# Attention values with V as the weight operand, the two head groups in the two halves of the array's columns

## What is computed

```python
def block_attn(args):                      # one block of 128 queries, all heads
    i, qb, ib = args
    ...
    s_s = jnp.einsum('bqgrd,bgqkd->bqgrk', qb, ksel)
    p_s = masked_softmax(s_s, smask)
    o_s = jnp.einsum('bqgrk,bgqkd->bqgrd', p_s, vsel)
    ...
    s_w = jnp.einsum('bqgrd,bkgd->bqgrk', qb, kwin)
    p_w = masked_softmax(s_w, wmask[None, :, None, None, :])
    o_w = jnp.einsum('bqgrk,bkgd->bqgrd', p_w, vwin)
    return o_s, o_w
...
out = g[..., 0:1] * o_cmp + g[..., 1:2] * o_sel + g[..., 2:3] * o_win
```

## Time and profile before

| | us |
|---|---|
| median of 3 runs | 1659.43 |
| lowest, highest | 1656.99, 1665.18 |
| span of the profiled execution | 1660.4 |
| attention phase: first score matmul to last values matmul | 607.0 to 911.2 |
| PE busy in the whole span | 1436.3 (87%) |

### The profile page before, as it was taken

How to read it: one execution, slowest core, us unless ns; L and a number is a source line. 1 busy time by engine, 2 the same in 40 slices (tenths; PEclk the granted TensorE clock), 3 DMA queues, 4 the chain that set the end, 5 groups by cost and what they waited for, 6 DMA issues and landing times. The chain is left out here.

```text
span 1660.4 us, 17595 instructions
## 1 busy us (share of the span) xinstructions
PE 1436.3 (87%) x6162; PEld 885.5 (53%) x6182; DVE 573.4 (35%) x1140; ACT 402.3 (24%) x990; POOL 193.0 (12%) x242
## 2 busy tenths in 40 slices
PE   4899999999967768999999599999729999999980
PEld 2445544554534667788887255566514444444440
DVE  0234223323345326655554113334551111111115
ACT  1121112111112534554443013233201111111110
POOL 0012012201210002111100000000011110110104
PEclk8899999999988658999999699999859999999995
DMA  9110001001207620100040310210155999999948
GB/s 366 47 38 26 19 32 38 25 13 38 64 31 260 230 70 26 52 27 27 24 193 8 118 51 4 73 39 26 39 177 189 366 372 364 372 371 365 370 151 304
DMA packets 125755, 224.16 MB, mean 135 GB/s; under 512 B 6016, under 2 KB 82048, under 8 KB 125568
## 3 DMA queue, kind: packets, MB, share of 16 engines
q1 hardware_dynamic: 118640, 197.69, 33.9%
q0 software_dynamic: 7056, 25.69, 4.1%
HBM read 181.42 MB, written 41.94 MB: 135 GB/s over the span
## 5 line engine op out<-in xcount | busy, mean ns | idle before, releaser
L432 PE MATMUL pj<-arena,xT 128*128 128x512 f32 (+1 forms) x768 | 318.5, 572 | 2.2 <-DMA arena<-in_w_in 2.0
L432 PEld LDWEIGHTS pj<-arena,xT 128*128 128x128 f32 x768 | 146.3, 194 | 155.4 <-issue 150.2
L1709 PE MATMUL egu<-arena,exT 128*128 128x512 f32 x512 | 227.6, 598 | 1.2 <-issue 1.2
L1709 PEld LDWEIGHTS egu<-arena,exT 128*128 128x128 f32 x512 | 95.7, 192 | 110.4 <-issue 109.8
L1108 DVE TENSOR_REDUCE anm<-asc 128x1 f32<-128x640 f32 (+7 forms) x128 | 90.5, 707 | 121.9 <-PE asc L1012 121.2
L1069 ACT ACTIVATE ap<-asc,anm 128x640 f32<-128x640 f32 (+7 forms) x128 | 89.7, 701 | 157.9 <-DVE anm L1108 147.4
L1697 PE MATMUL eyp<-arena,ehT 128*128 128x512 f32 x256 | 115.2, 593 | 1.0 <-ACT ehT L1740 1.0
L1267 PE MATMUL xpj<-arena,xTA 128*128 128x512 f32 x256 | 113.9, 604 | 0.7 <-ACT xTA L1334 0.7
L233 ACT ACTIVATE raw<-pj 128x512 f32<-128x512 f32 (+1 forms) x48 | 27.1, 564 | 271.9 <-PE pj L432 271.9
L1767 DVE TENSOR_TENSOR eh<-esg,egu 128x256 f32<-128x256 f32 x32 | 13.5, 421 | 220.2 <-ACT esg L1746 220.2
L1023 PE MATMUL atp<-early,ap 128*128 128x128 f32 x528 | 82.9, 281 | 5.1 <-ACT apT L1080 4.4
(11 more groups left out here) (321 smaller groups left out, 1978.2 us busy)
## 6 DMA issues: line engine op xcount, KB each, us to landing
arena<-in_w_gate SPq DMA_DIRECT2D x32, 1024.0 KB, 7.5
arena<-in_w_up SPq DMA_DIRECT2D x32, 1024.0 KB, 9.8
arena<-in_w_down SPq DMA_DIRECT2D x32, 1024.0 KB, 11.6
y_d<-ey SPq DMA_DIRECT2D x32, 512.0 KB, 9.9
arena<-in_w_in SPq DMA_DIRECT2D x6, 2048.0 KB, 18.6
x<-in_x SPq DMA_DIRECT2D x16, 512.0 KB, 4.2
y_d<-arena SPq DMA_DIRECT2D x2, 4096.0 KB, 18.7
rope<-in_rope SPq DMA_DIRECT2D x8, 512.0 KB, 3.5
```

Of the source, the lines that this page charges most:

```text
L432: last = nc.tensor.matmul(dst[:, 0:n], xT[:, k, :], w[c][:, k, :], start=k == 0, stop=k == KT - 1)
L1709: last = nc.tensor.matmul(gu[k % 2][:], xT[k % 2][:, c, :], m.gateup[k][:, c, :], start=c == 0, stop=c == KT - 1)
```

## The change

The product of probabilities and V is turned round. V is now the weight operand, 64 columns wide, and the transposed probabilities, 128 columns, move. The output is therefore transposed too: channels on partitions, queries along the row. A head of group 0 writes partitions 0 to 63 of `aov[branch]` and the head of group 1 at the same place p in its group writes partitions 64 to 127, so the two are products in different halves of the array's columns, and they are issued in turns (block 0 of group 0, block 0 of group 1, block 1 of group 0, ...).

For that the list of units changes: head pairs p = 0 to 3, and for each pair selected group 0, selected group 1, window group 0, window group 1. `values` handles two units at a time: PE does scores(u), turn(u - 2), and at even u values of units u - 4 and u - 3. `apT` has four buffers instead of two (two lie in `m.kcvcT`).

Because the output is transposed, it has to be turned back once a tile: `keep` copies `aov[0]` (ACT) and `aov[1]` (DVE) to `m.middle`, behind exponential or maximum of the tile's fourth unit (of the next tile) and ahead of the copies of unit u - 2; `turn_back` (PE) transposes the eight 128x128 blocks into two further pieces of `atp`, in the iteration after; `gates` reads those pieces instead of `aov`, two units later than before. Per-branch semaphores `a_kept` take the place of `a_read`, `a_free` that of `a_evac`.

```diff
 def attention_units():
 
     for i in range(NT):
-        for h in range(NH):
-            yield i, h, 0, 0, i + 1
-            yield i, h, 1, max(0, i - 4), min(i + 1, 5)
+        for p in range(HPG):
+            for branch, k0, n in ((0, 0, i + 1), (1, max(0, i - 4), min(i + 1, 5))):
+                for g in range(NG):
+                    yield i, g * HPG + p, branch, k0, n
...
-        pT = [sb(f"apT{b}", [P, NT, P]) for b in range(2)]
+        pT = [sb(f"apT{b}", [P, NT, P])[:] for b in range(2)]
+        pT += [m.kcvcT[:, b].rearrange("p (k q) -> p k q", k=NT) for b in range(2)]
+        oT = [m.middle[:, 512 * b:512 * b + 512] for b in range(2)]
...
+        first_piece, back_piece, f = {}, {}, 0
+        for u in range(U + 3):
+            if u < U:
+                first_piece[u] = f
+                f += len(pieces[u])
+            i, since = divmod(u - 2, PER)
+            if i >= 1 and since == 0:
+                back_piece[i - 1] = f
+                f += 2
+        after = lambda u: first_piece[u] + len(pieces[u])
...
-                def values(u):
-                    i, h, branch, k0, n = units[u]
+                def turn_back(i):
+
+                    for branch in range(2):
+                        f = back_piece[i] + branch
+                        pe.wait_ge(kept[branch], i + 1)
+                        pe.wait_ge(freed[f % 2], f // 2)
+                        for p in range(HPG):
+                            last = nc.tensor.transpose(tp[f % 2][:, p * P:(p + 1) * P],
+                                                       oT[branch][:, p * P:(p + 1) * P], m.c("ident"))
+                        last.then_inc(s["turned"], 1)
+
+                def values(j):
+
+                    i, p, branch, k0, n = units[2 * j]
                     v = m.vw if branch else m.vs
-                    g = h // HPG
-                    f = first_piece[u + 1]
-                    pe.wait_ge(s["evac0"], (f + 1) // 2)
-                    pe.wait_ge(s["evac1"], f // 2)
-                    if h == 0 and i:
-                        pe.wait_ge(s["read"], 2 * i)
+                    f = after(2 * j + 1)
+                    pe.wait_ge(freed[0], (f + 1) // 2)
+                    pe.wait_ge(freed[1], f // 2)
+                    if p == 0 and i:
+                        pe.wait_ge(kept[branch], i)
                     for b in range(n):
-                        at = (k0 + b) * P + g * HD
-                        last = nc.tensor.matmul(ov[branch][:, h * HD:(h + 1) * HD], pT[u % 2][:, b, :],
-                                                v[:, at:at + HD], start=b == 0, stop=b == n - 1)
+                        for g in range(NG):
+                            at = (k0 + b) * P + g * HD
+                            last = nc.tensor.matmul(ov[branch][g * HD:(g + 1) * HD, p * P:(p + 1) * P],
+                                                    v[:, at:at + HD], pT[(2 * j + g) % 4][:, b, :],
+                                                    start=b == 0, stop=b == n - 1)
                     last.then_inc(s["valued"], 1)
 
-                for u in range(U + 3):
+                for u in range(U + 5):
                     if u < U:
                         scores(u)
                     if 2 <= u < U + 2:
                         turn(u - 2)
-                    if u >= 3:
-                        values(u - 3)
-
...
+            def evacuate(eng, copy, u, parity):
                 for j, (k, n) in enumerate(pieces[u]):
                     f = first_piece[u] + j
                     if f % 2 == parity:
                         eng.wait_ge(s["turned"], f + 1)
-                        if u >= 2:
-                            eng.wait_ge(s["valued"], u - 1)
-                        copy(pT[u % 2][:, k:k + n, :],
-                             tp[f % 2][:, 0:n * P].rearrange("p (k q) -> p k q", k=n)).then_inc(sem_, 1)
+                        if u >= 4:
+                            eng.wait_ge(s["valued"], u // 2 - 1)
+                        copy(pT[u % 4][:, k:k + n, :],
+                             tp[f % 2][:, 0:n * P].rearrange("p (k q) -> p k q", k=n)).then_inc(freed[parity], 1)
+
+            def keep(eng, copy, i, branch):
+                eng.wait_ge(s["valued"], NH * (i + 1))
+                if i:
+                    eng.wait_ge(s["turned"], back_piece[i - 1] + branch + 1)
+                copy(oT[branch][:], ov[branch][:]).then_inc(kept[branch], 1)
...
+                copy = lambda o, a: nc.scalar.activation(o, a, ACT.Copy)
+                for u in range(U + 4):
                     if u < U:
                         softmax(u)
-                    if u >= 2:
-                        evacuate(act, lambda o, a: nc.scalar.activation(o, a, ACT.Copy), u - 2, 0, s["evac0"])
+                    i, since = divmod(u - 3, PER)
+                    if i >= 1 and since == 0:
+                        keep(act, copy, i - 1, 0)
+                    if 2 <= u < U + 2:
+                        evacuate(act, copy, u - 2, 0)
...
-                    dve.wait_ge(s["valued"], PER * (i + 1))
...
-                    nc.vector.tensor_tensor(heads(t1[:]), heads(ov[0][:]), bc(w[b][:, 0:8].unsqueeze(2), [P, NH, HD]),
-                                            ALU.mult).then_inc(s["read"], 1)
-                    nc.vector.tensor_tensor(heads(t2[:]), heads(ov[1][:]), bc(w[b][:, 8:16].unsqueeze(2), [P, NH, HD]),
-                                            ALU.mult).then_inc(s["read"], 1)
+                    for branch, t in enumerate((t1, t2)):
+                        f = back_piece[i] + branch
+                        dve.wait_ge(s["turned"], f + 1)
+                        nc.vector.tensor_tensor(
+                            t[:].rearrange("p (g h d) -> p g h d", g=NG, h=HPG),
+                            tp[f % 2][:].rearrange("p (h g d) -> p g h d", g=NG, h=HPG),
+                            bc(w[b][:, 8 * branch:8 * branch + 8].rearrange("p (g h o) -> p g h o", g=NG, o=1),
+                               [P, NG, HPG, HD]), ALU.mult).then_inc(freed[f % 2], 1)
...
-                for u in range(U + 3 + STEPS):
+                copy = lambda o, a: nc.vector.tensor_copy(o, a)
+                for u in range(U + 5 + STEPS):
                     if u < U:
                         maximum(u)
+                    i, since = divmod(u - 3, PER)
+                    if i >= 1 and since == 0:
+                        keep(dve, copy, i - 1, 1)
                     if 2 <= u < U + 2:
-                        evacuate(dve, lambda o, a: nc.vector.tensor_copy(o, a), u - 2, 1, s["evac1"])
-                    i, since = divmod(u - 2, PER)
+                        evacuate(dve, copy, u - 2, 1)
+                    i, since = divmod(u - 4, PER)
```

More of the change, by code:

```diff
@@ L947, in phase_attend @@
         pieces = [[(k, min(4, n - k)) for k in range(0, n, 4)] for _, _, _, _, n in units]
-        first_piece = [0]
-        for p in pieces:
-            first_piece.append(first_piece[-1] + len(p))
-        ocv = m.oc_d.rearrange("(t p) d -> t p d", p=P)
         U = len(units)
         PER = 2 * NH
+        first_piece, back_piece, f = {}, {}, 0
[8 more added lines that the diff above has]
+        after = lambda u: first_piece[u] + len(pieces[u])
+        ocv = m.oc_d.rearrange("(t p) d -> t p d", p=P)
         with nc.Block() as block:
@@ L1046, in _ @@
                         turn(u - 2)
-                    if u >= 3:
-                        values(u - 3)
-            def evacuate(eng, copy, u, parity, sem_):
+                    i, since = divmod(u - 4, PER)
+                    if i >= 1 and since == 0:
+                        turn_back(i - 1)
+                    if u >= 4 and u % 2 == 0 and u - 4 < U:
+                        values((u - 4) // 2)
+            def evacuate(eng, copy, u, parity):
                 for j, (k, n) in enumerate(pieces[u]):
@@ L1065, in softmax @@
                     if u >= 2:
-                        act.wait_ge(s["turned"], first_piece[u - 1])
+                        act.wait_ge(s["turned"], after(u - 2))
                     if h == 0 and i >= 2:
@@ L1131, in finish @@
                     if step == 1:
-                        dve.wait_ge(s["read"], 2 * i + 2)
+                        for branch in range(2):
+                            f = back_piece[i] + branch
+                            dve.wait_ge(freed[f % 2], f // 2 + 1)
                         done(nc.vector.tensor_tensor(t1[:], t1[:], t2[:], ALU.add))
```

8 lines of the change are left out of this document (5 added, 3 removed).

## The result

The changed kernel takes 1669.97 us in the median (1657.22 to 1676.33, 20 runs). The kernel before, in the same runs, takes 1656.93 (1651.14 to 1665.18, 20 runs). The ratio is 1.0077, with a 95% interval of 1.006 to 1.0095: slower by 13 us, where the forecast was 1668.3 and slower by 0.5% or a little more.

What follows compares the result with a forecast made beforehand. PE's own queue was taken to set the attention's pace before the change, with turns then waiting on ACT's copies. Terms -5 - 5.2 + 15.5 + 1 + 1.6 = +7.9 on 1660.4 gave 1668.3 us, range 1658 to 1680.

Steps and rivals of the forecast that it cites:

- part 1: Value matmuls: two streams run side by side in the array's halves, so 113 us become 56.5.
- The rival in which the halves take turns: Value matmuls: halves take turns or loads don't hide, 56 us more on PE, 1700 to 1725; chance 0.07.
- part 2: Around each of 64 values groups: entering and leaving the half-array form costs 0.3 us, 19 us in all.
- part 3: Turns in tiles 4 to 7 wait for ACT's copy to free `atp`; with the halved values, together -5.2 us.
- part 4: Seven tile borders: stalls and transposes for turning back, 19.7 us less 4.2 that go, +15.5 us.
- the gates' 4.2: Tile borders: the 4.2 us the first values waited for the gates in six borders before, expected to go.
- the pitch's 1.6: Value matmuls: the moving side at 0.11 instead of 0.107 on 528 steps adds 1.6 us.
- a rival of its own: Attention: border stalls and half-array products bring the lower clock, 1680 to 1695 us; chance 0.16.
- One sign of being wrong: Attention: a granted clock of 0.5 after tile 1, listed among what would show the forecast wrong.
- The cover holds: Attention turns don't wait, so PE's work decides: 30 us less, 1630 to 1648; chance 0.12.
- Borders are cheap: Tile borders: transposes back slip in without the 2 us stalls, sum -5, 1655 us; chance 0.09.
- the first list: Signs of being right: turn waits some 1.8 us, values groups 1.9 to 2.1, border idle about 2, copy waits near 45.

Runs made afterwards that it cites:

- the pair of kernels without stalls: New unit order with the old product, and the changed kernel without the turn back, both with ACT copying ahead of the exponential: 1646.62 and 1607.9 us.
- the second profile: The changed kernel, unedited, run and profiled once more: 1665.76 us, ratio 1.0054 to the kernel before.
- The swap: ACT's copy of unit u - 2 put ahead of the exponential of unit u: 1616.87 us on the changed kernel, 1643.26 on the kernel before.
- Kernels with half-array products and no stalled turns: The changed kernel with ACT copying ahead of the exponential, with and without the turn back: 1616.87 and 1607.9 us.
- a kernel with full-array products and the stalls: Kernel before with the new unit order, four apT buffers and values two units at a time, old product, no turn back: 1698.42 us, ratio 1.0258.

## Why the prediction was right

**What bounds.** The reading that ACT's copy, not PE's work, would set the pace holds: taking its cause away gives 49 to 53 us, and PE had 25 us less to do in a phase that grew.

**The values (part 1).** Taken: 0.107 to 0.11 for two instructions side by side. Measured 0.055 an instruction. The rival in which the halves take turns is out for the kernel as changed; it comes nearly true when the program order doesn't alternate. The Trainium skill (TensorE: Matmul & The Clock Gate, The mechanism) has weight loads overlap only where the row group differs. Here both halves use all rows and 32 matmuls with a load each still take 1.90 where the old form takes 3.49; the measurement decides.

**The change of form (part 2).** Taken 0.3 a group. The line through the two groups (1.24 for 20, 1.90 for 32) leaves 0.14 at none; and from a turn of 5 to the values are 0.67 (895.23 to 895.90) where the earlier trace rows have 0.57. That is 0.24 in sum. Parts 1 and 2 together were to save 37; the pair of kernels without stalls shows 38.7, up to 3.4 of it the clock.

**The turn's buffers (part 3).** The walk's 13.2 for four units of tile 7 is 13.23; in tile 4, walked at 10.98, four units take 11.05.

**The borders (part 4).** Taken 15.5; the kernel without the turn back is 17.5 faster. The stall was 1.93 for 2.1. The kernel without the turn back also has 7 to 10 us less at half the clock, up to 3.4 to 5.1 us, which is enough for the excess but was not separated from it.

By tiles, the whole of the forecast against the profile (the gates' 4.2 spread over the seven borders, the pitch's 1.6 apart):

| | tile 0 | 1 to 3 | 4 | 5 | 6 | 7 | end |
|---|---|---|---|---|---|---|---|
| forecast | 0 | -0.8 | +3.9 | +2.4 | +0.7 | -0.9 | +1 |
| measured | -0.7 | -0.5 | +4.6 | +2.4 | +0.8 | +3.5 | +0.8 |

**The term that was mis-sized** is the clock. The forecast had nothing for it and gave it a rival of its own, at 12 to 27 us. It was neither: 13.7 us more at half speed than before, in which PE was busy for 13.0, so 6.5 us at most (in the second profile 17.1 more, busy for 15.8, so 7.9 at most). The tiles' sum lies 4.6 above the forecast's terms (10.9 less 6.3), nearly all of it in tile 7 (4.4). There the clock accounts for 3.1 at most (6.20 us busy at 0.50), and the rest goes with an end that I had walked as if it were the middle. The last turn and the last values have no scores ahead of them any more, and wait (the turn 1.61 where the middle of the tile has 0.16):

```profile
908.47 0.73 PE L1034 MATMUL atp<-early,ap 128*128 128x128 f32 x5 [1.61 <-ACT apT L1109]
...
912.38 1.31 PE L1061 MATMUL aov<-kcvcT,vw 128*64 128x128 f32 x20 [0.58 <-ACT kcvcT L1109]
```

The rival was to decide as soon as most borders show 0.5. It was three of seven in the first profile and four of seven in the second, and the time was still not 1680: a stretch costs half its length at most, and 17 to 20 us of them cost 10 at most, not 12. One sign of being wrong, a clock of 0.5 after tile 1, thus came, and it marked the term that was left out and not a wrong mechanism. The forecast's 1.6 for the pitch is real (0.11), and the smaller change of form stands against it. And what was forecast against the profile's span and what was measured as a median agree to 1.7 us by luck: the phase alone says +11 to +13 where +7.9 was forecast, and the span of 1660.4 that it was added to lies 3.5 above the 20-run median of 1656.93. Counted from that median the forecast is 1664.8, 5.1 below what was measured.

**The rivals.** *The cover holds* was refuted in the kernel as changed and describes the one with ACT's copies first: there PE's work decides. It named 1630 to 1648 for that, and it is 1616.87. The swap also gives 14 us in the kernel before, by waits (and one stretch at the half clock) that this kernel had already; the rival had left them in. *Borders are cheap* fell with 1.93 us of stall. Of the signs that were named, all of the first list came: turns after window scores waiting 1.74, values groups of 1.90, PE idle 1.6 to 1.9 before the turn back into tiles 4 to 7 (in tiles 1 to 3 in two waits, 0.9 to 1.9 together), and 44.5 us of waits for the copies (near 45 said).

The Trainium skill (TensorEngine Tiling (Array Packing), PSUM Bottleneck) says that after a fourfold speed-up by packing the copy out of PSUM may become the bottleneck. The packing here is twofold, and the trace agrees in part: the copy was what PE waited for (44.5 us), yet ACT was busy for 147 of 331 us, and the same copies by the same engine in another place of its queue took the waits away.

## What to carry to other kernels

A matmul form that makes PE's groups shorter also takes cover away from the round trip that frees a PSUM buffer. Before such a change, walk one period with the round trip (maximum, exponential, copy, semaphore) and see which engine's queue order sets it; a copy that another engine waits for belongs ahead of work that only its own engine needs. Here the change and the swap together give 0.9756, the change alone 1.0077, the swap alone 0.9909. Two products in the two column halves should alternate instruction by instruction: half after half the changed kernel took 1703.88 instead of 1665.76 to 1669.97.

## What the runs showed of the hardware

- Two products with 64 weight columns each, in different column halves, run side by side with their weight loads: 0.055 us an instruction against 0.107, when they alternate. The reach is short: issued half after half, a group of 20 takes 1.95 us instead of 1.24, an overlap of 3 to 4 instructions by estimate.
- The lower clock followed stalls, not the kind of product. Kernels with half-array products and no stalled turns (two of them) had no stretch at 0.50 between tile 0 and the last values; a kernel with full-array products and the stalls had 23.9 us, more than the changed kernel's 17.1 and 20.5. With the copies first that full-array kernel kept 6.8 us, in tiles 1 and 3, where PE still waits for scores or values. What exactly decides at which stall the clock falls was not settled: the stretches lie at other places in two profiles of the same kernel.
- A wait costs more than the idle time that the trace gives for it: some 0.15 us of the matmul ahead of it, otherwise hidden under the next, comes to light. One turn showed it (a delay of 1.89 for 1.74 idle); over the whole phase it is worked out from sums.
